# Latent attention: four offset steps per item, values of half the queries in three pieces, the rotary key made once for all heads

## The reference, cut to what matters

```python
def _mla_queries(a_q, q_a_norm, w_uq, q_norm, rope):
    q = (_rms_norm(a_q, q_a_norm) @ w_uq).reshape(B, L, MLA_HEADS, QK_HEAD_DIM)   # 16 heads of 96
    q = _rms_norm(q, q_norm)
    q = jnp.concatenate([q[..., :QK_NOPE_DIM], _rope_2d(q[..., QK_NOPE_DIM:], rope)], axis=-1)

def _mla_keys_values(a_kv, kv_a_norm, w_ukv, k_norm, rope):
    ckv = _rms_norm(a_kv[..., :KV_LORA_RANK], kv_a_norm)
    k_pe = a_kv[..., KV_LORA_RANK:]                                               # 32 wide, one for all heads
    kv = (ckv @ w_ukv).reshape(B, L, MLA_HEADS, QK_NOPE_DIM + V_HEAD_DIM)
    k_nope, v = kv[..., :QK_NOPE_DIM], kv[..., QK_NOPE_DIM:]
    k_pe = jnp.broadcast_to(k_pe[:, :, None, :], (B, L, MLA_HEADS, QK_ROPE_DIM))
    k = _rms_norm(jnp.concatenate([k_nope, k_pe], axis=-1), k_norm)               # then rotated, as q

s = jnp.einsum('bqhd,bkhd->bhqk', qblk, k) * scale
p = jax.nn.softmax(s, axis=-1)
o = jnp.einsum('bhqk,bkhv->bqhv', p, v)
```

## Time and profile before

| | |
|---|---|
| median of 3 runs | 3585.41 us (3578.99 to 3586.26) |
| the profiled execution | 3582.74 us, its span 3581.0 us |
| low-rank end and first four heads | 1036.00 to 1091.96 us of the span |
| items 0 to 63 and their values | 1091.96 to 1408.18 us |
| the output projection's first matmul | 1408.18 us |

### The profile page before, as it was taken

The page is one execution under the profiler, slowest core; times in us unless marked ns, Lnnn a source line. Parts: engine busy times, 40 slices in busy tenths (PEclk is TensorE's granted clock), DMA queues, the critical chain, the costliest instruction groups (busy, mean ns, idle before and its releaser), DMA issues.

```text
span 3581.0 us, 39546 instructions
## 1 busy us (share of the span) xinstructions
PE 3307.6 (92%) x15924; PEld 2595.4 (72%) x15924; DVE 1475.7 (41%) x2561; ACT 1328.2 (37%) x2324; POOL 1438.9 (40%) x814
## 2 busy tenths in 40 slices
PE   7999999999987887999989898899998989889998
PEld 4855788888844454788876687678887667768886
DVE  5557332222247663321224647342323555734142
ACT  4222332222235554332333524343333453434243
POOL 2224432232423333444461146644465025564446
PEclk9999999999998998999999999999999999999999
DMA  5144212112240000323232020323332212022322
GB/s 223 59 143 170 94 61 70 59 57 69 64 164 15 13 12 14 128 82 113 78 110 89 24 78 1 116 83 89 106 89 88 66 53 69 14 82 91 104 86 67
DMA packets 85635, 286.03 MB, mean 80 GB/s; under 512 B 9772, under 2 KB 10348, under 8 KB 84941
## 3 DMA queue, kind: packets, MB, share of 16 engines
q1 hardware_dynamic: 85452, 283.50, 24.1%
HBM read 281.37 MB, written 2.10 MB: 79 GB/s over the span
## 4 chain that ended last, share of the span: by engine, by line
PE 82%; DVE 10%; ACT 5%; DMA 2%; issue 1%; POOL 0%; SPq 0%; DVEq 0%; ACTq 0%
PE ps L444 20%; PE ps L447 19%; PE ps L445 19%; PE ps L469 2%; PE ps L471 2%; PE ps L470 2%; DMA ring<-in_w_mod 2%; PE ps L1980 2%; PE ps L493 1%; DVE T L2624 1%; DVE sm L1923 1%; PE ps L1140 1%; PE ps L1913 1%; PE ps L2296 1%; PE ps L415 1%
## 5 line engine op out<-in xcount | busy, mean ns | idle before, releaser
L389 POOL TENSOR_TENSOR WL<-ring,WH 128x1024 fp32r<-128x1024 f32 (+2 forms) x443 | 958.9, 2168 | 1566.1 <-ACT WH L380 1565.5
L444 PE MATMUL ps<-HX,WH 128*128 128x512 f32 x1768 | 694.4, 393 | 3.8 <-POOL WL L389 3.8
L447 PE MATMUL ps<-HX,WL 128*128 128x512 f32 x1768 | 691.9, 391 | 0.0
L445 PE MATMUL ps<-HX,WH 128*128 128x512 f32 x1768 | 690.4, 390 | 0.0
L380 ACT CAST WH<-ring 128x1024 fp32r<-128x1024 f32 (+2 forms) x443 | 420.6, 951 | 424.9 <-PE ps L447 326.9
L444 PE MATMUL ps<-FR,WH 128*128 128x512 f32 x1120 | 418.3, 373 | 0.0
L445 PE MATMUL ps<-FR,WH 128*128 128x512 f32 x1120 | 409.5, 373 | 0.0
L444 PEld LDWEIGHTS ps<-HX,WH 128*128 128x128 f32 x1768 | 332.4, 188 | 81.4 <-issue 5.7
L447 PE MATMUL ps<-FR,WL 128*128 128x512 f32 x1120 | 389.2, 373 | 0.0
L447 PEld LDWEIGHTS ps<-HX,WL 128*128 128x128 f32 x1768 | 333.7, 189 | 49.6
L445 PEld LDWEIGHTS ps<-HX,WH 128*128 128x128 f32 x1768 | 332.5, 188 | 49.1
(11 more groups left out here) (378 smaller groups left out, 5255.1 us busy)
## 6 DMA issues: line engine op xcount, KB each, us to landing
ring<-in_w_mod SPq DMA_DIRECT2D x96, 512.0 KB, 5.6
ring<-in_ffn_w_up SPq DMA_DIRECT2D x88, 512.0 KB, 3.3
ring<-in_w_up SPq DMA_DIRECT2D x88, 512.0 KB, 3.2
ring<-in_w_in_tok SPq DMA_DIRECT2D x40, 512.0 KB, 3.3
ring<-in_w_in_feat SPq DMA_DIRECT2D x32, 512.0 KB, 3.2
ring<-in_ffn_w_down SPq DMA_DIRECT2D x32, 384.0 KB, 3.1
ring<-in_w_out SPq DMA_DIRECT2D x32, 384.0 KB, 3.1
ring<-in_w_down SPq DMA_DIRECT2D x32, 384.0 KB, 3.1
```

Of the source, the lines that this page charges most:

```text
L389: pool.tensor_tensor(WL[:, p % SPLITS, 0:n], ring.ap(r), WH[:, p % SPLITS, 0:n], ALU.subtract).then_inc(*ring.frees(r, split.g, "low", p))
L444: pe.matmul(o, high, xh, k == 0, False)
L445: pe.matmul(o, high, xl, False, False)
L447: m = pe.matmul(PS[bs[i]][:, 0:N], low, get(k)[0], False, k == g.kt - 1)
```

## The change

- The order of an engine's step is now `scores(i)`, `turn(i-3)`, one part of `values`, one piece of `beside`, `high(i-55)`. On VectorE `scores(i)` is `sum(i-2)` and `max(i)`; on ScalarE `exp(i-1)`; on GpSimd `scale(i-2)`. The loop has 71 steps.
- Items are ordered so that every four items are two heads with half the queries. Values of such a half (`v`, 0 to 15) are 256 columns, in three parts of two key tiles, in three successive steps. Their PSUM bank is held for the whole loop (`hold`), so the other seven go round.
- `kpe` is squared, summed, given its gain and rotated once in `low_rank_v`. The sum (`epsk`) enters the means of the keys; the key squares, reductions and scalings are 64 wide per head, and one multiplication writes the rotary part of each head from `kpe` and the factor. The copies of `kpe` and the rotation of keys per four heads are gone.
- `rkv` is made by `inverse_root_v` instead of ScalarE's square root and a reciprocal; `small` is marked after it.
- Queries are finished (factors, rotation) before the key work. Pieces of `beside` run in steps 1 to 15 of each sixteen; kv comes two pieces later; heads are turned one per step, and scores wait only for their own head (`made`, n, h).

```diff
+    def hold(self, *key):
+        b = next((x for x in self.kept if self.holder[x][0] == key[0]), None)
+        if b is None:
+            b = self.take(*key)
+            self.kept.add(b)
+            return b
+        self.former[key], self.holder[b], self.place[key] = self.holder[b], key, b
         return b
...
         def low_rank_v(dve):
...
+            inverse_root_v(dve, mla, rkv, mkv, scratch24[:, 0:6], 1.0)
+            mla.v.mark("small")
...
+            dve.tensor_tensor(squares, kpe, kpe, ALU.mult).then_inc(*mla.v.up())
+            dve.wait_ge(*mla.v.now())
+            dve.tensor_reduce(epsk, squares, AX, ALU.add).then_inc(*mla.v.up())
+            dve.tensor_tensor(kpe, kpe, rows[:, 160:192].unsqueeze(1).to_broadcast([128, 6, 32]), ALU.mult).then_inc(
+                *mla.v.up())
+            dve.wait_ge(*mla.v.now())
+            dve.tensor_scalar(epsk, epsk, 1.0 / 96, EPS, ALU.mult, ALU.add).then_inc(*mla.v.up())
+            dve.wait_ge(*lds["rope"])
+            rope_v(dve, kpe[:, 0:4, :].unsqueeze(2), 1, 0)
...
         def heads_v(dve, n):
             yield
-            kpe_v(dve, n)
             yield
             mean_v(dve, n, 0)
             yield
             mean_v(dve, n, 1)
             query_v(dve, n, 0)
             yield
+            query_v(dve, n, 1)
+            query_factors_v(dve, n)
+            yield
+            rope_v(dve, qtok.rearrange("p t (h c) -> p t h c", h=4), 4, 64)
+            yield
             mean_v(dve, n, 2)
-            query_v(dve, n, 1)
             yield
             mean_v(dve, n, 3)
             yield
             mean_v(dve, n, 4)
             key_factors_v(dve, n)
             yield
-            dve.wait_ge(*lds["rope"])
-            rope_v(dve, qtok.rearrange("p t (h c) -> p t h c", h=4))
             key_v(dve, n, 2)
+            key_v(dve, n, 3)
             yield
-            key_v(dve, n, 3)
             key_v(dve, n, 4)
-            yield
-            rope_v(dve, ktok[:, 0:4, :].rearrange("p t (h c) -> p t h c", h=4))
-            query_factors_v(dve, n)
             mla.v.mark("heads", n)
...
         def item(i):
             n, j = divmod(i, 16)
-            return n, j // 4, j % 4
+            return n, j // 8 * 2 + j // 2 % 2, j // 4 % 2 * 2 + j % 2
...
+        def lat_values_pe(pe, v, part):
+            n, q = v // 4, v // 2
+            c0 = v % 2 * 256
+            if part == 0 and v % 2 == 0:
+                bank.hold("lv", q)
+                pe.wait_ge(*bank.free("lv", q))
+            if part == 0:
+                pe.wait_ge(*att.a.at("turned", 4 * v + 3, 1))
+            o = ps("lv", q)
+            for j in range(2 * part, 2 * part + 2):
                 for x in range(2):
-                    c = (2 * two + x) * 64
-                    m = pe.matmul(PS[b][64 * x:64 * x + 64, :], VT[n % 2][:, j, c:c + 64], PT[x][:, j, :], j == 0, j == 5)
-            m.then_inc(*att.pe.up("values", q))
+                    c = (q % 2 * 2 + x) * 64
+                    m = pe.matmul(o[64 * x:64 * x + 64, c0:c0 + 256], VT[n % 2][:, j, c:c + 64], PT[x][:, j, c0:c0 + 256],
+                                  j == 0, j == 5)
+            if part == 2:
+                m.then_inc(*att.pe.up("values", v))
...
-            for i in range(68):
+            for i in range(71):
+                if i < 64 and i % 16 == 0:
+                    last_of(beside)
+                    beside = heads(i // 16 + 1) if i < 48 else iter(())
+                scores(i)
+                if 0 <= i - 3 < 64:
+                    turn(i - 3)
+                if i >= 7:
+                    values(*divmod(i - 7, 4))
+                if i % 16 >= 1:
+                    next(beside, None)
+                if 55 <= i < 62:
+                    high(i - 55)
```

More of the change, by code:

```diff
@@ L1728, in heads_pe @@
                     yield
+            for _ in range(2):
+                yield
             r = ring.raw(dr["mla_w_ukv"][n], 512)
@@ L1740, in heads_pe @@
                     yield
-            for _ in range(6):
+            for _ in range(4):
                 yield
@@ L1768, in heads_a @@
                     yield
+            for _ in range(2):
+                yield
             act.wait_ge(*mla.v.at("small"))
             if n >= 2:
-                act.wait_ge(*att.pe.at("values", 2 * n - 3))
+                act.wait_ge(*att.pe.at("values", 4 * n - 5))
             for t in range(6):
@@ L1970, in lat_turn_a, with lat_values_a @@
                     *bank.emptied(("lt", i, x), att.a, "turned", i, x))
[L1972 to L1984 removed]
+        def lat_values_pe(pe, v, part):
[8 more added lines that the diff above has]
+            for j in range(2 * part, 2 * part + 2):
+                for x in range(2):
+                    c = (q % 2 * 2 + x) * 64
[3 more added lines that the diff above has]
+                m.then_inc(*att.pe.up("values", v))
+        def lat_values_a(act, v, part):
+            if part < 3 or v % 2 == 0:
+                return
+            q = v // 2
+            act.wait_ge(*att.pe.at("values", v))
             if q < 6:
@@ L2011, in latent @@
             beside = iter(())
-            for i in range(68):
-                if i < 64:
-                    if i % 16 == 0:
-                        last_of(beside)
-                        beside = heads(i // 16 + 1) if i < 48 else iter(())
-                    scores(i)
-                if i >= 10 and (i - 3) % 8 == 7:
-                    values((i - 3) // 8)
-                if 0 <= i - 2 < 64:
-                    turn(i - 2)
-                if i % 16 >= 3:
-                    next(beside, None)
-                if 54 <= i < 60:
-                    high(i - 54)
@@ L2031, in latent_v, with latent_pe, scores, values @@
+        def latent_pe(pe):
+            def scores(i):
+                if i < 64:
+                    lat_scores_pe(pe, i)
+            def values(v, part):
+                if v < 16 and part < 3:
+                    lat_values_pe(pe, v, part)
+            latent(lambda n: heads_pe(pe, n), adaln_pe(pe, range(18, 22)), scores, lambda i: lat_turn_pe(pe, i), values,
+                   Nothing())
+            bank.kept.clear()
         def latent_v(dve):
             def scores(i):
-                if i:
-                    lat_sum_v(dve, i - 1)
@@ new lines, in scores, with values, high @@
+                if i < 64:
+                    lat_max_v(dve, i)
+            def values(v, part):
+                if part == 3 and v in (13, 15):
+                    lat_low_v(dve, v // 2)
+            def high(k):
+                if k:
+                    lat_low_v(dve, k - 1)
+            latent(lambda n: heads_v(dve, n), adaln_v(dve, range(18, 22)), scores, Nothing(), values, high)
+        def latent_a(act):
+            def scores(i):
+                if 0 <= i - 1 < 64:
+                    lat_exp_a(act, i - 1)
+            def high(k):
+                if k < 6:
+                    lat_high_a(act, k)
+            latent(lambda n: heads_a(act, n), adaln_a(act, range(18, 22)), scores, lambda i: lat_turn_a(act, i),
+                   lambda v, part: lat_values_a(act, v, part), high)
```

134 lines of the change are left out of this document (50 added, 84 removed).

## The result

The changed kernel takes 3532.78 us (median of 4 runs, 3531.52 to 3536.59), the kernel before 3585.84 (4 runs beside it): a ratio of 0.9856, 95% interval 0.9839 to 0.9873. The forecast was 3526, its range 3498 to 3560. The profiled execution took 3533.16 us, its span 3531.4.

The account below looks back on a forecast made before the run. The stage was taken as bound by waits, no engine being full. Savings of 26.1 (middle), 4.5 (start) and 28.1 (tail), 58.7 us from 3582.74, give 3524.0, named 3526 because the median is 2.7 above the profiled run; range 3498 to 3560.

Parts of the forecast that it names:

- (c): Item loop: an item's whole path becomes one circle through the held bank, 4.9 us a step, 3612 us; chance 0.05.
- (d): Item loop: no change, values hide nothing because the path stays on VectorE; chance 0.03.
- Rival (a): Items 0 to 48: TensorE's lead buffers VectorE's heavy steps, stretches cost 59 to 60 us, total 3494; chance 0.12.
- Rival (b): Items 0 to 48: seven banks and exponentials behind head copies add 0.8 us a heavy step, total 3552; chance 0.22.
- Tail: Item 48 to the output projection: 56 us against 84.1, 28.1 saved, bounds 18 and 32.
- Start: Before item 0: first head turned at about 1079.6 instead of 1084.13, 4.5 us saved, bounds 0 and 6.
- Middle: Items 0 to 48: stretches of 66, 70 and 70 us, together 206 against 232.1, 26.1 saved.
- The hand-over, -2.0: Step 12 of a sixteen-item stretch: TensorE already has most of its items' part done, 2.0 us less.
- The bank wait behind the key and value copies: Steps 5 to 7: two copies a tile make scores wait 0.9 us, covered by VectorE; uncovered, 3 x 0.9 more.
- the cut item circle: Item loop: VectorE and ScalarE work at once, so 3.40 us an item becomes the busiest engine's 2.74.
- Crossings: Values on TensorE: entering and leaving the two-column-half form, 0.1 us each, 8 us in all, some 5 where TensorE binds.
- The key work: VectorE's head making: 7.3 us removed per four heads, of it six copies 2.2 and the key's rotation 3.2.

Follow-up runs that it names:

- the best kernel here: Changed kernel with ScalarE's head copies one step later, behind the exponential, and the held bank last in the bank order when the loop ends: 3505.97 us.
- The offsets: Alone: changed kernel with the old item order and values as 24 passes of 512 columns every eight items, later exp, sum, scale and transposes kept: 3523.33 us.
- halves: Alone: changed kernel with exp, sum, scale and transposes back in their old steps, values of half the queries kept: 3523.71 us.
- late copies: Changed kernel with ScalarE's copies for the next heads one step later, behind the exponential: 3511.66 us.
- without either item edit: Changed kernel with old steps for exp, sum, scale and transposes, old item order and values as 24 passes of 512 columns: 3547.20 us.
- the spread: Kernel before with head-making pieces in steps 1 to 15 instead of 3 to 15, heads turned one a step instead of two: 3576.86 us.
- the key work put back: Changed kernel with six copies of `kpe` and one spare rotation per four heads added on VectorE: 3548.35 us.

## Why the prediction was right, and where its steps were not

**The total** was right to 7 us, and the change faster as said, but the middle's part of it came by another way than the one argued; rivals (c), slower, and (d), no change, are out. Rival (a), full overlap with the middle at 177 us, didn't come, and isn't reached by the best kernel here either (188.4). Its total of 3494 takes 91 us as saved where its middle and the prediction's own start and tail give 87.7, which is 3498. Rival (b) had the right mechanism, the exponential queued behind the head copies, at a price too high for this kernel: 228 us for the middle, measured 211.1, forecast 206.

**Tail: right.** Forecast 56, measured 57.2. The fifteen steps came to 43.6 us (forecast 43.5) and what follows item 63 to 13.6 (forecast 12.5, and under 13 as a sign of being right). The 1.5 us in which the projection waits for the remainder of values 7 are in it and were not in the sum; the 1.5 that the sum had, for values 6, took 1.2 in the chain (1346.85 to 1348.07). The offsets cut the circle there, as argued: 76.5 to 62.9 alone, 65.9 to 57.2 with halves.

**Start: right.** 4.4 us against 4.5. Heads are first turned 50.6 us after the first `stat` matmul instead of 54.1; the line itself is near 1084, not near 1080, because this trace was 3.6 us late before.

**Middle: 5.1 us short, and for the wrong reason.** The stretches 16 to 48 were put at 70, measured 73.5 each; the first was put at 66 and took 64.1. Two terms of the sum failed. *The hand-over, -2.0*: step 12 wasn't shorter, it was the longest (6.23). Steps 12 to 15 and 0 to 2, with all their stalls, take 36.6 us, where the terms came to 35.2 (28.9 + 5.8 + 1.0 + 1.5 - 2.0, the 28.9 being 29.2 when its own parts are added up); the 1.5 for a lower clock weren't lost either, for it was 1.00. *The bank wait behind the key and value copies, said to lie "in steps 5 to 7, where VectorE is later anyway"*: these steps take 15.9 us, and 13.5 with late copies and the same work on VectorE, so the wait was not covered. Steps 3 to 11 took 36.9 instead of 34.4. In all, a stretch has 9.7 us of waits for exponentials where 5.8 were charged. The error was to take, step by step, the busier of two engines. ScalarE's copies wait for TensorE, the exponential for the copies, TensorE for the exponential: in such a circle the works of the engines add up. The waits of 1.2 us behind a turned head were seen and sized well (1.22 before the scores at 1212.82), but counted as a surcharge on TensorE's sum and not as what makes the rest of the step unhidden.

**What the middle was won by.** The prediction put the cut item circle first. The experiments put it last: without either item edit the middle is at 206.3 us already, of which the spread gives 9.3 (232.1 to 222.8) and the rest of the change 16.5. That rest, the lighter key work, the new order of the head pieces, the held bank and what the clock gave, was not split up. The two item edits together then cost 4.8 there, and give 19.3 in the tail. So that the forecast of the middle came within 5.1 us is in part luck: the gain was there, but the term to which it was put down took some away.

**Crossings: nearly right.** 0.2 us a piece was charged; it is 0.25 to 0.30. The Trainium skill, "TensorEngine Tiling", section "Key Properties", says that changing the tiling mode drains TensorE; the trace has a price at these changes, 0.25 to 0.30 us a piece; whether it is a drain, no run shows. The pairs of passes are 0.21 apart (1316.21 to 1316.42), their weight loads hidden, so the upper bound of 12 us didn't come.

**The key work** was priced too high: the six copies, put at 2.2 us, keep VectorE busy for 0.9; with the other terms as they stand, 6.0 us were removed per four heads and not 7.3. The rotation was priced rightly (3.2, measured 3.1), and that it would be on the path in step 12, where TensorE was taken to bind, was not seen.

## What to carry to other kernels

Before a step's cost is taken as that of its busiest engine, follow each bank or buffer that is taken again to its last reader, and see what is queued ahead of that reader on its own engine: where this leads back to the engine that waits, the step costs the sum. An instruction that frees a bank for another engine belongs ahead of copies that nobody needs yet; here that one move was worth 22.8 us, nearly half as much as the whole change. And two edits that each take away the same stop must be measured together: here they gave 22.5 and 18.0 us of the stage alone and 14.5 together, and both became worth having only after a third. Last, when an experiment adds work, look at which steps grow and at their clock before the cost is put down to the work.

## What the runs showed that was not expected

- Of the 4.9 us that the key work put back costs in a middle stretch, 2.9 are TensorE's own work at a clock of 0.50.
- In the traces read here TensorE's clock fell behind stops: it is 1.00 in every stretch of the changed kernel, with waits of at most 1.4 us. With the key work back TensorE waits 1.84 us and soon after 1.37, the clock falls to 0.50 at 1218.33 for 6.8 us, and the middle stretches show 0.95 and 0.96. With neither item edit, where TensorE stops for the last `PT` copy, it is 0.95 and 0.98 in two stretches alike in work, and 0.93 in the tail:

```profile
1161.11:1232.17 71.06, 63.73 (x276) 35.62 (x276) 47.91 (x138) 44.41 (x121) 29.50 (x21) 0.95 0.05 16
1232.17:1303.24 71.07, 62.67 (x277) 34.48 (x277) 47.92 (x138) 44.42 (x121) 29.50 (x21) 0.98 0.04 15
...
1303.24:1379.70 76.46, 58.72 (x244) 29.00 (x245) 34.31 (x91) 43.27 (x115) 24.92 (x17) 0.93 0.00 0
```

  The two stretches take the same time (71.06 and 71.07) at different clocks: there TensorE's speed was not what bound them.
